# Second block's attention over even and odd tokens, four heads in a row

## The chip, the cores and the metric

One core of one Trainium2 chip runs the program. The metric is the device time of one execution in microseconds; of several executions the median is given. Shorter is better.

## What is computed

The program computes two transformer-like blocks over one sequence of 256 tokens of width 1024. The change touches only the second block's attention: three groups of 8 heads (head size 64), each with its own window and dilation.

```python
DILATED_GROUPS = ((128, 1), (512, 4), (2048, 16))      # (window, dilation)

def dilated_window_attention(q, k, v, window, dilation):
    """query t attends keys t, t-d, ..., t-(window//d)*d"""

def hybrid_mixer(x, w_in, conv_w, conv_b, conv_ln_g, conv_ln_b, w_attn_out, w_conv_out, w_o):
    h = x @ w_in
    ...
    gates = jax.nn.sigmoid(h[..., QKV_COLS + 2 * CONV_CHANNELS:])
    g_attn, g_conv = jnp.split(gates, 2, axis=-1)
    for g, (window, dilation) in enumerate(DILATED_GROUPS):
        q = apply_rotary(qkv[:, :, g, 0], cos, sin)
        k = apply_rotary(qkv[:, :, g, 1], cos, sin)
        o, lse = dilated_window_attention(q, k, qkv[:, :, g, 2], window, dilation)
    ...                                   # the groups are joined by softmax over lse
    y_attn = o.reshape(B, S, ATTN_WIDTH) @ w_attn_out
    u = a * jax.nn.sigmoid(b)             # a, b: the rest of h
    u = conv(u) + conv_b                  # 31 taps, one filter per channel
    u = jax.nn.silu(layer_norm(u, conv_ln_g, conv_ln_b))
    y_conv = u @ w_conv_out
    return (g_attn * y_attn + g_conv * y_conv) @ w_o
```

Joining the groups by their log-denominators equals one softmax over the keys of all three groups together, and this is how the kernel computes it. In the second and third group a query sees only keys at a distance that is a multiple of 4 or 16, so an even token sees even tokens alone there and an odd one odd tokens alone.

## The kernel before

Each engine has a program of its own, written in the order in which it runs; semaphores join them. TensorE (PE) multiplies, ScalarE (ACT) applies functions and copies, VectorE (DVE) does arithmetic, GpSimd (POOL) little, SyncE (SP) issues the weight transfers. All products of activations with weights are done in three passes with operands split into a high and a low half: ACT rounds a weight chunk to its high half (L1053, `highs`), DVE subtracts it from the raw one (L1544, `lows`), PE multiplies high with high, high with low and low with high.

A small class (`Psum`) hands out the eight PSUM banks while the programs are written. `take` gives the bank that was handed out longest ago among those allowed (`low` is the lowest allowed, `at` asks for one bank), and returns what must be waited for: the reading of the result that lay there before. So whoever takes a bank waits for the engine that empties it.

The second block first computes its queries, keys and values with `lin_tm` (L459, matmuls L474 to L476): the stationary operand is a slice of 128 tokens of the activations (`hx`), the moving one 512 columns of weights. `turn` rotates q and k on DVE and POOL, PE transposes them (L880), ACT copies them to `Q2` and `K2`.

Then comes a loop of 20 steps, one for each of the 16 pairs (query tile `qb`, head `h`) in `ITEMS2` and four to drain. The query tile 0 is tokens 0 to 127, tile 1 tokens 128 to 255. In step i:

- PE: `scores2` for the heads i and i+1 if i is even (L906): three groups by two heads, of 128 key columns for tile 0 and 256 for tile 1. `turned2(i-3)` (L916): 3 or 6 transposes of the probabilities. `values2(i-5)` if i is odd (L931): 6 or 12 matmuls for two heads. Then the fill of the step: `FILL` holds 16 gate projections (24 matmuls each, L384 to L389) for steps 0 to 15 and 8 of `conv_out` (12 each) from step 16 on, the last two of them after the loop. In steps 4, 8 and 9 there are small matmuls for the convolution's layer norm (L939, L527, L533).
- ACT: `pt2(i-3)` copies the transposed probabilities out of PSUM (L1420), `exps2(i)` (L1414) applies exp and sums, then `highs` of a later weight chunk (L1053) and the tanh of the gate (L1406), which frees its bank.
- DVE: `maxes2(i)` adds the mask and takes the maximum (L2120), then scales it by -0.125 (L2123); `norm2(i-1)` (L2130, L2132) divides by the sum; in the first steps the rest of the convolution taps (L2077); `lows` of a later chunk (L1544); parts of the layer norm (`rstd` L1585 to L1589 in step 8) and for `conv_out` L2143.

```python
    for i in range(20):
        if i < 16 and i % 2 == 0:
            scores2(i)
        if 0 <= i - 3 < 16:
            turned2(i - 3)
        if i >= 5 and i % 2:
            values2(i - 5)
        ...
        for what, m in fills(i):
            (gate if what == "gate" else conv_out)(m, None if i < 8 or i > 15 else 6 if i < 13 else 7)
```

The output of a query tile gathers in one PSUM bank (`o2`, held from h = 0 to h = 6) and is split by ACT (`out2`, L1425) and DVE (L2137). Behind the loop PE projects it (`ao`, L968 to L970), DVE merges with the gates (L2212, L2215, L2206), ACT rounds (L1477), and PE goes on with `w_o` (L367 to L371).

The first block's attention, in `layer`, has a loop of its own, with scores of four heads in a row in the banks 0 to 3, `turned` (L781) with 4 transposes for each item of its second layer, and `values` (L796) for two heads at a time with 8 matmuls for each pair.

Of the kernel before, what the change touches and what calls it, by code (L numbers as in the profile page):

```python
# [31 lines left out]
def const_layout():  # L32
# [8 lines left out]
        ("mask1", 3 * 256),  # L41
# [163 lines left out]
def geometry(K):  # L205
# [64 lines left out]
    g.P2 = area(4 * 768)  # L270
    g.rot = g.P2
    g.P2T = area(4 * 768)
# [73 lines left out]
def tensor_program(K, e):  # L346
# [112 lines left out]
    def lin_tm(key, wname, l, cols, n, xh, xl, tiles, per, xw, side=None, mid=None, chunk=1):  # L459
# [4 lines left out]
        for g in range(0, KD, per):  # L464
# [418 lines left out]
    for gi in range(3):  # L883
        for w in range(3):
            last = (gi, w) == (2, 2)
            lin_tm(("qkv", gi, w), "w_in_2", 0, (gi * 1536 + w * 512, 512), 512, x2h, x2l, [0, 1], 2, xt, mid=heads2 if last else None, chunk=2)
            if late:
                heads2()
            if w < 2:
                late.append((gi, w))  # L890

    def gate(m, at):
        lin(("gate", m), "w_in_2", 0, (4608 + 1024 + P * m, P), range(KD), x2h, x2l, 256, xt, at)

    def conv_out(m, at=None):
        lin(("cout", m), "w_conv_out_2", 0, (P * m, P), range(4), lambda k: K.ch[:, k, :], lambda k: K.cl[:, k, :], 256, lambda k: V["ch", k], at)

    def scores2(i):

        qb, h = ITEMS2[i]  # L900
        w = (qb + 1) * P
        pe.wait_ge(A["heads2"], *(x for y in range(2) for x in ps.take(("s2", i + y), 1 + qb, at=2 * y if qb else None)))
        for gi in range(3):
            for y in range(2):
                r = slice(64 * y, 64 * y + 64)
                n = e.matmul(ps.ap(("s2", i + y), w, gi * w), g.Q2[r, gi, h // 2, qb * P:(qb + 1) * P], g.K2[r, gi, h // 2, 0:w], start=True, stop=True, skip_group_check=True)  # L906
        n.then_inc(*M.up(("s2", i)))

    def turned2(i):
        qb = ITEMS2[i][0]  # L910
        n = 3 * (qb + 1)
        key = ("p2T", i)
        pe.wait_ge(V["p2", i], *ps.take(key, 1 + qb, at=4 if qb else None))
        for j in range(n):
            o = i % 4 * 768 + j * P
            k = e.transpose(ps.ap(key, P, j * P), g.P2[:, o:o + P], C("ident"))  # L916
        k.then_inc(*M.up(key))

    def values2(i):

        qb, h = ITEMS2[i]
        nb = qb + 1
        key = ("o2", qb)
        if h == 0:
            pe.wait_ge(*ps.take(key, hold=True, at=7 - qb))
        pe.wait_ge(A["p2t", i + 1], A["v2"])
        for j in range(3 * nb):
            for y in range(2):
                o = ps.ap(key, P, (h // 2) * P, slice(64 * y, 64 * y + 64))
                pt = (i + y) % 4 * 768 + j * P  # L930
                n = e.matmul(o, g.V2[:, j % nb, j // nb, (h + y) * 64:(h + y + 1) * 64], g.P2T[:, pt:pt + P], start=j == 0, stop=j == 3 * nb - 1, skip_group_check=True)  # L931
        n.then_inc(*M.up(("pv2", i)))
        if h == 6:
            M.mark(key)
            ps.drop(key)
# [5 lines left out]
    for i in range(20):  # L941
        if i < 16 and i % 2 == 0:
            scores2(i)
        if 0 <= i - 3 < 16:
            turned2(i - 3)
        if i >= 5 and i % 2:
            values2(i - 5)
# [7 lines left out]
        for what, m in fills(i):  # L955
            (gate if what == "gate" else conv_out)(m, None if i < 8 or i > 15 else 6 if i < 13 else 7)
# [84 lines left out]
def scalar_program(K, e):  # L1041
# [367 lines left out]
    def exps2(i):  # L1409
        w = 3 * (ITEMS2[i][0] + 1) * P  # L1410
        z = i % 4
        pb = g.P2[:, z * 768:z * 768 + w]
        ac.wait_ge(V["max2", i])
        e.activation(pb, pb, ACT.Exp, bias=g.st2[:, z:z + 1], scale=0.125, accum_out=g.st2[:, 4 + z:5 + z]).then_inc(*A.up(("exp2", i)))  # L1414

    def pt2(i):
        n = 3 * (ITEMS2[i][0] + 1) * P
        y = i % 4
        ac.wait_ge(M["p2T", i], M["pv2", (i - 4) // 2 * 2] if i >= 4 else None)
        e.activation(g.P2T[:, y * 768:y * 768 + n], ps.ap(("p2T", i), n), ACT.Copy).then_inc(*A.up(("p2t", i)))  # L1420
        ps.give(("p2T", i), A.now())

    def out2(qb):
# [1228 lines left out]
```

## Time and profile before

| | |
|---|---|
| median of 3 runs | 871.27 us (869.71 to 871.9) |
| the profiled execution, its own time | 870.63 us |
| its span, first to last instruction | 868.7 us |
| PE busy | 845.6 us (97%) |
| DVE busy | 624.5 us (72%) |
| ACT busy | 446.9 us (51%) |
| mean granted TensorE clock | 0.996 of full speed |

The span is what the profile explains; 1.9 us of the execution's time lie around it. PE is nearly always busy, so what counts is PE's work in a stage and the places where PE waits. The loop of 20 steps runs from 545.37 us to 633.46 us of the span. Shapes in the rows are partitions x elements; in the profile each matmul of attention in plain fp32 (L906, L931, L796) stands as two records, so 6 matmuls are "x12".

### The profile page before, as it was taken

The numbers are of one execution on the slowest core, as the hardware profiler recorded it, in microseconds if no ns is written. First come the engines' busy times: TensorE is split into PE (matmuls) and PEld (weight loads), VectorE is DVE, ScalarE is ACT, GpSimd is POOL, SyncE is SP. The second block draws the span as 40 slices with busy tenths as digits, with TensorE's granted clock in tenths as the row PEclk, the third lists the DMA queues.
The fourth block names the chain that finished last, engine by engine and source line by source line (L and its number), as shares of the span: only waits on it lengthen the run. The fifth ranks groups of instructions, "written<-read, shape, count | busy, mean of one in ns | idle before, by whom it ended". The sixth has DMA issues, their size and how long they took to land.

```text
span 868.7 us, 13531 instructions
## 1 busy us (share of the span) xinstructions
PE 845.6 (97%) x5432; PEld 701.5 (81%) x5432; DVE 624.5 (72%) x1242; ACT 446.9 (51%) x782; POOL 23.4 (3%) x19
## 2 busy tenths in 40 slices
PE   7999999999999999999999999999999999999996
PEld 4668567776876888769988888998999988888885
DVE  4544867867456779875699999977598766565665
ACT  3352636645433565764444444666653765555552
POOL 0000000000000000000003113000000000000000
PEclk9999999999999999999999999999999999999999
DMA  9785542301173035222655665532456365655541
GB/s 353 311 309 194 218 182 97 110 2 61 62 276 117 24 106 175 74 98 97 215 182 164 197 199 163 167 123 60 127 190 236 105 209 172 213 170 193 195 168 49
DMA packets 40718, 138.27 MB, mean 159 GB/s; under 512 B 4432, under 2 KB 4560, under 8 KB 40400
## 3 DMA queue, kind: packets, MB, share of 16 engines
q1 hardware_dynamic: 40224, 134.41, 45.7%
q10 hardware_dynamic: 432, 3.00, 0.9%
q8 instruction: 43, 0.70, 0.3%
q14 instruction: 19, 0.16, 0.1%
HBM read 136.34 MB, written 1.05 MB: 158 GB/s over the span
## 4 chain that ended last, share of the span: by engine, by line
PE 83%; DVE 8%; DMA 3%; ACT 3%; issue 1%; SPq 1%; POOLq 0%; DVEq 0%; POOL 0%; ACTq 0%
PE ps L429 9%; PE ps L1013 6%; PE ps L384 5%; PE ps L385 5%; PE ps L474 5%; PE ps L476 5%; PE ps L475 5%; PE ps L430 4%; PE ps L389 4%; PE ps L773 2%; PE ps L781 2%; DMA AF<-wmod 2%; PE ps L796 2%; DVE wlo L1544 2%; PE ps L504 2%; PE ps L401 2%
## 5 line engine op out<-in xcount | busy, mean ns | idle before, releaser
L1053 ACT ACTIVATE whi<-raw 128x1024 fp32r<-128x1024 f32 (+3 forms) x213 | 211.6, 1003 | 102.2 <-DMA raw<-wpack 56.4
L1544 DVE TENSOR_TENSOR wlo<-raw,whi 128x1024 fp32r<-128x1024 f32 (+3 forms) x213 | 240.9, 1154 | 27.5 <-ACT whi L1053 27.3
L384 PE MATMUL ps<-hx,whi 128*128 128x256 f32 (+1 forms) x384 | 115.5, 301 | 0.0
L429 PE MATMUL ps<-hx,whi 128*128 128x512 f32 x320 | 113.8, 398 | 0.0
L385 PE MATMUL ps<-hx,whi 128*128 128x256 f32 (+1 forms) x384 | 112.1, 292 | 0.0
L389 PE MATMUL ps<-hx,wlo 128*128 128x256 f32 (+1 forms) x332 | 97.0, 292 | 0.0
L430 PE MATMUL ps<-hx,wlo 128*128 128x256 f32 x320 | 89.8, 281 | 0.0
L384 PEld LDWEIGHTS ps<-hx,whi 128*128 128x128 f32 x384 | 73.4, 191 | 3.4 <-issue 1.9
L385 PEld LDWEIGHTS ps<-hx,whi 128*128 128x128 f32 x384 | 73.5, 191 | 2.0 <-issue 0.7
L474 PE MATMUL ps<-whi,hx 128*128 128x512 f32 (+1 forms) x192 | 71.8, 374 | 0.9 <-DVE lat L1680 0.9
L429 PEld LDWEIGHTS ps<-hx,whi 128*128 128x128 f32 x320 | 60.2, 188 | 14.5
L475 PE MATMUL ps<-wlo,hx 128*128 128x512 f32 (+1 forms) x192 | 71.0, 370 | 0.0
L476 PE MATMUL ps<-whi,hx 128*128 128x512 f32 (+1 forms) x192 | 71.0, 370 | 0.0
L389 PEld LDWEIGHTS ps<-hx,wlo 128*128 128x128 f32 x332 | 63.5, 191 | 1.1
L430 PEld LDWEIGHTS ps<-hx,wlo 128*128 128x128 f32 x320 | 60.5, 189 | 0.7
L2077 DVE SCALAR_TENSOR_TENSOR AF<-AF,cst 128x256 f32<-128x256 f32 x120 | 58.1, 532 | 0.4
L1013 PE MATMUL ps<-whi,hx 128*128 128x512 f32 x176 | 51.2, 392 | 0.0
L1301 ACT ACTIVATE AF<-ps,AF 128x512 f32<-128x512 f32 (+1 forms) x48 | 29.2, 613 | 29.0 <-DVE AF L1956 29.0
L474 PEld LDWEIGHTS ps<-whi,hx 128*128 128x128 f32 x192 | 36.7, 191 | 6.6 <-DVE lat L1680 1.1
L2297 DVE TENSOR_TENSOR AF<-AF,ps 128x256 f32<-128x256 f32 x20 | 8.4, 422 | 45.8 <-ACT AF L1514 45.8
L476 PEld LDWEIGHTS ps<-whi,hx 128*128 128x128 f32 x192 | 36.7, 191 | 5.6
L475 PEld LDWEIGHTS ps<-wlo,hx 128*128 128x128 f32 x192 | 36.8, 192 | 5.4
(326 smaller groups left out, 1649.4 us busy)
## 6 DMA issues: line engine op xcount, KB each, us to landing
raw<-wpack SPq DMA_DIRECT2D x181, 512.0 KB, 4.0
AF<-wmod SPq DMA_DIRECT2D x48, 512.0 KB, 6.4
raw<-wpack SPq DMA_DIRECT2D x24, 256.0 KB, 3.4
raw<-wpack SPq DMA_DIRECT2D x6, 384.0 KB, 3.4
XT<-xin SPq DMA_DIRECT2D x4, 512.0 KB, 6.2
raw<-wpack SPq DMA_DIRECT2D x4, 432.0 KB, 5.0
cst<-cpack ACTq DMA_DIRECT2D x1, 1349.0 KB, 9.0
AF<-l2rows ACTq DMA_DIRECT2D x1, 1024.0 KB, 6.8
```

The lines of the kernel that those rows point to most:

```text
L384: e.matmul(o, wh[:, b], xh(k), start=j == 0, stop=False, skip_group_check=True)
L385: e.matmul(o, wh[:, b], xl(k), start=False, stop=False, skip_group_check=True)
L389: e.matmul(o, wl[:, b], xh(k), start=False, stop=False, skip_group_check=True)
L429: e.matmul(ps.ap(key, 512).rearrange("p (s n) -> p s n", s=2), wh[:, b], K.hx[:, :, k, 0:256], start=k == 0, stop=False, skip_group_check= ...
L430: i = e.matmul(ps.ap(key, 256), wl[:, b], hh[:, k, 0:256], start=False, stop=k == KD - 1, skip_group_check=True)
L474: e.matmul(o, xh(k)[:, ts], wh[:, b], start=k == 0, stop=False, skip_group_check=True)
L475: e.matmul(o, xh(k)[:, ts], wl[:, b], start=False, stop=False, skip_group_check=True)
L476: i = e.matmul(o, xl(k)[:, ts], wh[:, b], start=False, stop=k == KD - 1, skip_group_check=True)
L1013: i = e.matmul(ps.ap(("fd", t), 512, 512 * q), y[:, f % 8, x], w[:, 512 * q:512 * q + 512], start=f == 0 and y is K.fh and w is wh, stop=f ...
L1053: e.activation(W.hi(i), W.raw(i), ACT.Copy).then_inc(*HI.up(j))
L1544: e.tensor_tensor(W.lo(i), W.raw(i), W.hi(i), ALU.subtract).then_inc(*LO.up(j))
L2077: e.scalar_tensor_tensor(out=g.CV[:, m, :], in0=g.U[:, m, j:j + 256], scalar=w, in1=g.CV[:, m, :], op0=ALU.mult, op1=ALU.add).then_inc(*V. ...
```

## The change

Queries are taken as even tokens (tile t = 0) and odd tokens (t = 1), and so are keys: `lin_tm` gets `parity=True` for q, k and v and loads every second column of the activations as its stationary operand. In the second and third group a query needs only the keys of its own parity, in the first group all 256. Every item so has 256 + 128 + 128 = 512 key columns, where it had 384 for the first tile and 768 for the second. The scores of an item fit in one bank.

- `scores2` now does four heads in a row (12 matmuls), in steps 0, 4, 8 and 12, always into the banks 0 to 3. All else takes the banks 4 to 7 (`ps.low = 4`) until step 14.
- `turned2` has 4 transposes and follows one step later (i-4).
- `values2` has 8 matmuls for two heads; two calls stand together in the steps 8, 12, 16 and 19. The output is gathered for four heads in a bank and split four times (`out2(0)` to `out2(3)`), written to every second column of `oh` and `ol`.
- DVE takes four maxima in a row; the scaling by -0.125 goes into the same instruction (scale -0.125 and minimum), so L2123 goes. `norm2(i)` follows in the same step. ACT's exponentials and copies get the order of the first block's loop.
- `P2` has 8 buffers of 512 instead of 4 of 768. The masks take 640 columns in place of 768 in the constants, and the rotary tables are laid out by parity.

```diff
@@ lin_tm
-                    ts = slice(t * P, (t + 1) * P)
+                    ts = slice(t, 2 * P, 2) if parity else slice(t * P, (t + 1) * P)
...
     def scores2(i):
-        qb, h = ITEMS2[i]
-        w = (qb + 1) * P
-        pe.wait_ge(A["heads2"], *(x for y in range(2) for x in ps.take(("s2", i + y), 1 + qb, at=2 * y if qb else None)))
-        for gi in range(3):
-            for y in range(2):
...
+        t, h = ITEMS2[i]
+        pe.wait_ge(A["heads2"], *(x for j in range(4) for x in ps.take(("s2", i + j), at=j)))
+        for gi, at, n, first in ((0, 0, 256, 0), (1, 256, P, t * P), (2, 384, P, t * P)):
+            for j in range(4):
+                r = slice(64 * (j % 2), 64 * (j % 2) + 64)
+                m = e.matmul(ps.ap(("s2", i + j), n, at), g.Q2[r, gi, (h + j) // 2, t * P:(t + 1) * P], g.K2[r, gi, (h + j) // 2, first:first + n], start=True, stop=True, skip_group_check=True)
...
     def turned2(i):
-        pe.wait_ge(V["p2", i], *ps.take(key, 1 + qb, at=4 if qb else None))
-        for j in range(n):
+        pe.wait_ge(V["p2", i], *ps.take(key))
+        for j in range(4):
...
     def values2(i):
+        key = ("o2", i // 4)
+        if h % 4 == 0:
+            pe.wait_ge(*ps.take(key))
         pe.wait_ge(A["p2t", i + 1], A["v2"])
-        for j in range(3 * nb):
+        for j, (u, gi) in enumerate(((0, 0), (1, 0), (t, 1), (t, 2))):
...
     for i in range(20):
-        if i < 16 and i % 2 == 0:
+        ps.low = 4 if i < 15 else 0
+        if i < 16 and i % 4 == 0:
             scores2(i)
-        if 0 <= i - 3 < 16:
-            turned2(i - 3)
-        if i >= 5 and i % 2:
-            values2(i - 5)
+        if i >= 8 and i % 4 == 0:
+            values2(i - 8)
+            values2(i - 6)
+        if 0 <= i - 4 < 16:
+            turned2(i - 4)
+        if i == 19:
+            values2(12)
+            values2(14)
@@ scalar_program
-        if 0 <= i - 3 < 16:
-            pt2(i - 3)
-        if i < 16:
-            exps2(i)
+        for j in ((i, i + 1), (i + 1,), (i + 1,), ())[i % 4] if i < 16 else ():
+            exps2(j)
+        for j in ((), (i - 5,), (i - 5,), (i - 5, i - 4))[i % 4]:
+            if j >= 0:
+                pt2(j)
...
-        if i == 12:
-            out2(0)
+        if i in (8, 12, 16):
+            out2(i // 4 - 2)
@@ vector_program, maxes2
-        e.tensor_tensor_reduce(p3, s3, mk, 1.0, -3.0e38, ALU.add, ALU.max, mx).then_inc(*V.up())
+        e.tensor_tensor_reduce(p2, s2, mk, -0.125, 3.0e38, ALU.add, ALU.min, g.st2[:, z:z + 1]).then_inc(*V.up(("max2", i)))
         ps.give(("s2", i), V.now())
-        dv.wait_ge(V.now())
-        e.tensor_scalar(mx, mx, -0.125, None, ALU.mult, ALU.bypass).then_inc(*V.up(("max2", i)))
@@ vector_program, the loop
+        for j in range(i, i + 4) if i < 16 and i % 4 == 0 else ():
+            maxes2(j)
         if i < 16:
-            maxes2(i)
-        if 0 <= i - 1 < 16:
-            norm2(i - 1)
+            norm2(i)
```

Where the instructions stand. First ACT in the steps 4 and 5, before the change (L1420 is the copy `pt2`, L1414 the exponential, L1429 the mean, L1053 a high half, L1406 the tanh of a gate):

```order
L1420 ACTIVATE AF<-ps 128x384 [waits mm_done]
L1414 ACTIVATE AF<-AF 128x384 [waits dve_done]
L1429 ACTIVATE acc<-ps 128x256 [waits mm_done]
L1053 ACTIVATE whi<-raw 128x1024 [waits raw_in3]
L1406 ACTIVATE AF<-ps 128x256 [waits mm_done]
L1420 ACTIVATE AF<-ps 128x384 [waits mm_done]
L1414 ACTIVATE AF<-AF 128x384 [waits dve_done]
L1053 ACTIVATE whi<-raw 128x1024 [waits raw_in0]
L1406 ACTIVATE AF<-ps 128x256 [waits mm_done]
```

and in the changed kernel (L1413 is the exponential, L1418 the copy `pt2`, L1428 the mean):

```order
L1413 ACTIVATE AF<-AF 128x512 [waits dve_done] x2
L1428 ACTIVATE acc<-ps 128x256 [waits mm_done]
L1053 ACTIVATE whi<-raw 128x1024 [waits raw_in3]
L1406 ACTIVATE AF<-ps 128x256 [waits mm_done]
L1413 ACTIVATE AF<-AF 128x512 [waits dve_done]
L1418 ACTIVATE AF<-ps 128x512
L1053 ACTIVATE whi<-raw 128x1024 [waits raw_in0]
L1406 ACTIVATE AF<-ps 128x256 [waits mm_done]
```

Before, a step's copy came ahead of its exponential, and the copy of one item fell in the same step as its transposes. Now the exponential stands ahead of the copy, and the copy falls in the step after the transposes of its item, behind the tanh of the gate of that earlier step.

Next PE at the start of step 5 of the changed kernel: the last matmuls of the gate of step 4, the transposes, and the first matmuls of the gate:

```order
L385 MATMUL ps<-hx,whi 128x256
L387 MATMUL ps<-hx,wlo 128x256
L913 MATMUL ps<-cst,AF 128x128 [waits act_done]
L913 MATMUL ps<-cst,AF 128x128 x3
L384 MATMUL ps<-hx,whi 128x256 [waits act_done,w_low]
L385 MATMUL ps<-hx,whi 128x256
```

The gate of step 5 waits for ACT here: it takes the bank in which `turned2(0)` of step 4 lay. The gate of step 10 has the same wait, for the bank of `turned2(5)` of step 9. Then step 8 as a whole up to its gate (L905 is `scores2`, L927 `values2`, L913 `turned2`):

```order
L905 MATMUL ps<-AF 128x256 [waits dve_done]
L905 MATMUL ps<-AF 128x256 x3
L905 MATMUL ps<-AF 128x128 x8
L927 MATMUL ps<-AF 64x128 [waits act_done]
L927 MATMUL ps<-AF 64x128 x7
L927 MATMUL ps<-AF 64x128 [waits act_done]
L927 MATMUL ps<-AF 64x128 x7
L913 MATMUL ps<-cst,AF 128x128 [waits dve_done]
L913 MATMUL ps<-cst,AF 128x128 x3
L527 MATMUL ps<-cst,acc 128x1 [waits dve_done]
L527 MATMUL ps<-cst,acc 128x1
L384 MATMUL ps<-hx,whi 128x256 [waits act_done,w_low]
```

and the same step before:

```order
L906 MATMUL ps<-AF 128x256 [waits dve_done,act_done]
L906 MATMUL ps<-AF 128x256 x5
L916 MATMUL ps<-cst,AF 128x128 x3
L527 MATMUL ps<-cst,acc 128x1 [waits dve_done]
L527 MATMUL ps<-cst,acc 128x1
L384 MATMUL ps<-hx,whi 128x256 [waits act_done,w_low]
```

The scores of four heads and the values of four heads now stand in one step; the step after it has the transposes alone, with a wait for DVE (the bank of the output), and the small matmul of the layer norm with a wait for ACT (the bank of `turned2(4)`). Step 9 on PE in the changed kernel, with the end of the gate ahead of it and the start of its own:

```order
L385 MATMUL ps<-hx,whi 128x256
L387 MATMUL ps<-hx,wlo 128x256
L913 MATMUL ps<-cst,AF 128x128 [waits dve_done]
L913 MATMUL ps<-cst,AF 128x128 x3
L533 MATMUL ps<-wk,cst 128x256 [waits act_done]
L384 MATMUL ps<-hx,whi 128x256 [waits w_low]
```

The gate of step 9 has no wait for a bank left; the two waits stand ahead of it.

## Rows read from the trace of the kernel before

**Rows 1.** Busy time of the engines in the loop: us, then each engine's
```profile
545.37:633.46 88.09, 87.90 (x802) 81.97 (x801) 66.95 (x164) 54.68 (x106) 0.00 (x0) 1.00 0.38 120
```

**Rows 2.** The chain that ended last, 540 to 650: start, us, engine and line
```profile
540.00 0.23 PE ps L475
...
545.43 0.87 PE ps L906 x12
...
576.63 1.50 PE ps L906 x12
...
630.78 0.42 DVE AF L2143
631.20 0.60 DVE hx L2137
631.80 1.13 DVE wlo L1544
...
647.64 0.43 ACT hx L1477
```

**Rows 3.** PE in order of time, second gate of the loop: start, us
```profile
549.21 0.28 PE L384 MATMUL ps<-hx,whi 128*128 128x256 f32 x1
...
552.18 0.94 PE L906 MATMUL ps<-AF 64*128 64x128 f32 x12
```

**Rows 4.** PE in order of time, first block's second attention
```profile
363.88 0.60 PE L781 MATMUL ps<-cst,AF 128*128 128x128 f32 x4
364.24 0.36 PE L412 MATMUL ps<-hx,whi 128*128 128x256 f32 x1
364.44 0.28 PE L413 MATMUL ps<-hx,wlo 128*128 128x256 f32 x1
...
372.56 1.97 PE L796 MATMUL ps<-AF 128*64 128x128 f32 x32
374.46 0.66 PE L781 MATMUL ps<-cst,AF 128*128 128x128 f32 x4
374.87 0.36 PE L401 MATMUL ps<-hx,whi 128*128 128x256 f32 x1
```

**Rows 5.** DVE in order of time, in the loop
```profile
547.00 0.56 DVE L2120 CUSTOM_DVE_ANT_1 AF<-ps,cst 128x384 f32<-128x384 f32 x1
547.48 0.08 DVE L2120 DVE_READ_ACCUMULATOR2_ANT AF<- 128x1 f32 x1
547.60 0.15 DVE L2123 TENSOR_SCALAR AF<-AF 128x1 f32<-128x1 f32 x1
547.67 2.46 DVE L2077 SCALAR_TENSOR_TENSOR AF<-AF,cst 128x256 f32<-128x256 f32 x6
550.05 1.22 DVE L1544 TENSOR_TENSOR wlo<-raw,whi 128x1024 fp32r<-128x1024 f32 x1
...
578.17 0.96 DVE L2120 CUSTOM_DVE_ANT_0 AF<-ps,cst 128x768 f32<-128x768 f32 x1 [2.60 <-PE ps L906]
...
579.77 0.15 DVE L1585 TENSOR_SCALAR nrm<-ps 128x2 f32<-128x2 f32 x1
...
581.68 1.22 DVE L1544 TENSOR_TENSOR wlo<-raw,whi 128x1024 fp32r<-128x1024 f32 x1
```

**Rows 6.** ACT in order of time, in the loop
```profile
564.06 0.37 ACT L1406 ACTIVATE AF<-ps 128x256 f32<-128x256 f32 x1
564.37 0.49 ACT L1420 ACTIVATE AF<-ps 128x384 f32<-128x384 f32 x1
564.76 0.61 ACT L1414 ACTIVATE AF<-AF 128x384 f32<-128x384 f32 x1
565.27 0.19 ACT L1414 ACTIVATION_READ_ACCUMULATOR AF<-AF 128x1 f32 x1
565.36 1.05 ACT L1053 ACTIVATE whi<-raw 128x1024 fp32r<-128x1024 f32 x1
```

**Rows 7.** Line 474, its weight loads: ns min/median/max, first and last start
```profile
L474 PEld LDWEIGHTS ps<-whi,hx x192: 186/188/329, 69.6 to 544.4; 128*128 128x128 f32 x192
```

More of the change, by code:

```diff
@@ L919, in values2 @@
     def values2(i):
[L921 to L925, printed above, removed]
+        t, h = ITEMS2[i]
+        key = ("o2", i // 4)
+        if h % 4 == 0:
+            pe.wait_ge(*ps.take(key))
         pe.wait_ge(A["p2t", i + 1], A["v2"])
-        for j in range(3 * nb):
+        for j, (u, gi) in enumerate(((0, 0), (1, 0), (t, 1), (t, 2))):
             for y in range(2):
-                o = ps.ap(key, P, (h // 2) * P, slice(64 * y, 64 * y + 64))
-                pt = (i + y) % 4 * 768 + j * P
-                n = e.matmul(o, g.V2[:, j % nb, j // nb, (h + y) * 64:(h + y + 1) * 64], g.P2T[:, pt:pt + P], start=j == 0, stop=j == 3 * nb - 1, skip_group_check=True)
+                o = ps.ap(key, P, (h // 2) % 2 * P, slice(64 * y, 64 * y + 64))
+                pt = (i + y) % 4 * 512 + j * P
+                n = e.matmul(o, g.V2[:, u, gi, (h + y) * 64:(h + y + 1) * 64], g.P2T[:, pt:pt + P], start=j == 0, stop=j == 3, skip_group_check=True)
         n.then_inc(*M.up(("pv2", i)))
-        if h == 6:
+        if h % 4 == 2:
             M.mark(key)
-            ps.drop(key)
     def conv_sums():
@@ L955, in tensor_program @@
         for what, m in fills(i):
-            (gate if what == "gate" else conv_out)(m, None if i < 8 or i > 15 else 6 if i < 13 else 7)
+            (gate if what == "gate" else conv_out)(m)
     M.mark("attn2")
@@ L1468, in scalar_program @@
                 gate(m)
-    out2(1)
+    out2(3)
     for what, m in FILL[22:]:
@@ L2132, in norm2, with out2 @@
         e.tensor_scalar(pb, pb, sm, None, ALU.mult, ALU.bypass).then_inc(*V.up(("p2", i)))
-    def out2(qb):
-        dv.wait_ge(A["o2", qb])
-        c = slice(qb * P, (qb + 1) * P)
-        e.tensor_tensor(K.ol[:, :, c], ps.ap(("o2", qb)).rearrange("p (k n) -> p k n", k=4), K.oh[:, :, c], ALU.subtract).then_inc(*V.up("o2"))
-        ps.give(("o2", qb), V.now())
+    def out2(q):
+        dv.wait_ge(A["o2", q])
+        k, ts = slice(q % 2 * 2, q % 2 * 2 + 2), slice(q // 2, 2 * P, 2)
+        e.tensor_tensor(K.ol[:, k, ts], ps.ap(("o2", q), 256).rearrange("p (k n) -> p k n", k=2), K.oh[:, k, ts], ALU.subtract).then_inc(*V.up("o2"))
+        ps.give(("o2", q), V.now())
     def conv_out(m):
@@ L2558, in tables, with mask @@
     ang2 = (np.arange(256, dtype=f32)[:, None] * inv2[None]).astype(f32)
-    c["cos2"] = np.cos(ang2).astype(f32).reshape(2, 128, 32).transpose(1, 0, 2)
-    c["sin2"] = np.sin(ang2).astype(f32).reshape(2, 128, 32).transpose(1, 0, 2)
+    c["cos2"] = np.cos(ang2).astype(f32).reshape(128, 2, 32)
+    c["sin2"] = np.sin(ang2).astype(f32).reshape(128, 2, 32)
     c["nsin2"] = -c["sin2"]
-    t, s = np.arange(256)[:, None], np.arange(256)[None, :]
-    m = []
-    for win, dil in ((128, 1), (512, 4), (2048, 16)):
-        ok = (t >= s) & ((t - s) % dil == 0) & ((t - s) <= win)
-        m.append(np.where(ok, 0.0, NEG).astype(f32))
-    c["mask1"] = np.stack([x[128:, :] for x in m], 1)
+    def mask(a, b, win, dil):
+        t, s = 2 * np.arange(128)[:, None] + a, 2 * np.arange(128)[None, :] + b
+        return np.where((t >= s) & ((t - s) % dil == 0) & (t - s <= win), 0.0, NEG).astype(f32)
+    near = (128, 1)
+    c["mask1"] = np.stack([mask(1, 0, *near), mask(0, 0, *near), mask(0, 1, *near), mask(0, 0, 512, 4), mask(0, 0, 2048, 16)], 1)
     e = np.zeros((128, 4), f32)
```

62 lines of the change are left out of this document (27 added, 35 removed).

## Prediction

> **What bounds the kernel now.** I read first the busy times of the loop that the change rewrites: PE is busy 87.90 of its 88.09 us [rows 1], while DVE works 66.95 and ACT 54.68. So a matmul taken out of the loop is worth its full length, as long as nobody makes PE wait in its place. Then the chain that ended last [rows 2]: through the loop it is PE's own work; it leaves PE at 630.78, where DVE takes up the sixth `conv_out`, and stays on DVE up to 647.6 (the split of the output 0.60, low halves of 1.13, the merging), before ACT and PE's `w_o`. DVE's stretch starts from a result of PE, so what the loop gains or loses on PE is passed on whole. Then PE in order of time [rows 3, 4] for lengths of blocks, and DVE and ACT in order of time [rows 5, 6], because they empty the banks that PE takes.
>
> **PE's work after the change.** I build the new loop from blocks, each from the start of a block to the start of the next. Scores: 6 matmuls of 128 columns take 0.87, of 256 columns 1.50 [rows 2], so 0.145 and 0.25 each; a row of four heads is 4 x 0.25 + 8 x 0.145 = 2.16, four rows 8.6. Values: the first block already has exactly the new block (two pairs, 8 matmuls each, x32): 374.46 - 372.56 = 1.90 [rows 4]; four of them 7.6. Transposes: four in a row take 0.36 between projections, 0.41 behind values [rows 4]; 11 and 5 of them make 6.0. Projections: one gate with the switch to scores behind it took 552.18 - 549.21 = 2.97 [rows 3]; 24 matmuls at 0.12 are 2.88 of it and 0.09 is the switch. 16 gates and 8 `conv_out` of half the length are 57.6. The first projection matmul behind another kind takes 0.20 [rows 4] in place of 0.12: 17 such switches are 1.4. Seven switches into scores and values are 0.6. The three small groups of the layer norm stay as they are; what is left of the 88.09 once all old blocks are taken off gives them about 1.1 with their switches (0.33, 0.37 and 0.42, my division). Sum: 8.6 + 7.6 + 6.0 + 57.6 + 1.4 + 0.6 + 1.1 = 82.9. PE's work falls by 88.1 - 82.9 = **5.2 us**.
>
> **What PE then waits for.** Before, PE could take any bank; now steps 0 to 14 have four banks (4 to 7) for a transpose result, a gate, and now and then an output or a statistic. A bank comes back after four takes. In two steps this gives the gate of step i the bank of the transposes of step i-1: step 5 (bank of item 0) and step 10 (bank of item 5). The copy that empties it is on ACT, in step i, behind the tanh of the gate before and an exponential. ACT's prices [rows 6], start to start: tanh 0.27 to 0.31, exponential 0.51 + 0.09 at 384 columns (I take 0.72 at 512), copy 0.39 at 384 (0.50 at 512, both raised with the columns), high half 1.05 long, 0.95 to the next. DVE's [rows 5]: a maximum at 384 columns runs 0.48 and 0.12 more until its result can be used; at 768 its duration is 0.96 in place of 0.56, so at 512 one takes 0.61 + 0.12 = 0.735, four 2.95. The removed L2123 gives 0.07 of start to start.
>
> *Step 10*: the gate of step 9 ends at a time T. ACT sees it at T + 0.2 (a matmul lasts 0.28, and T is 0.12 from the last one's start [rows 3]), then tanh 0.27, exponential 0.72, copy 0.50, and 0.1 to PE: T + 1.8. PE has only four transposes (0.36) to do meanwhile. It waits **1.4**.
>
> *Step 5*: DVE is behind here. Before, it worked the six last taps (2.38) and a low half after one maximum; now it starts at 547.6 (first row of scores done, 545.37 + 2.16 + 0.1), and does 4 maxima 2.95, norm 0.59, taps 2.38, low 1.13, then norm, four taps 1.6, low, then norm, sums 1.6, low, then norm, low: it comes to the maxima of step 4 at 563.1, though PE has had those scores ready since 561.4. ACT: exponentials of items 4 and 5 from 563.9 to 565.3, mean 0.27, high half 0.95, tanh to 566.8, exponential of item 6 to 567.5, copy of item 0 to 568.0, PE at 568.1. PE comes there at 545.37 + 2.16 + 2.97 + 3 x 2.88 + 0.09 + 2.15 + 0.41 + 0.33 + 2.97 + 0.36 = 565.4. It waits **2.7**. Without DVE's delay it would be the 1.4 of step 10; that is the lower bound.
>
> *Step 9*: the transposes want the bank of the first output, which DVE empties only behind four maxima (2.95), norm 0.59 and the `rstd` of 1.91 (581.68 - 579.77 [rows 5]) and 0.36 for the split: 5.9 after the scores are seen. PE has values 1.90, transposes 0.41, the statistic 0.37 and a gate 2.97 = 5.65: it waits **0.4**. Behind it the layer norm's matmul wants the bank of item 4: T + 1.8 again, against 0.4 + 0.36 done: **1.0**. Sum of waits: 2.7 + 0.4 + 1.0 + 1.4 = **5.5 us**. In step 19 item 15's transposes stand next to the values that need them; its copy (0.50 and about 0.3 to see and be seen) is covered by `values2(12)` (0.95). Its bounds are 0 and 0.4; I take 0, as the copy before it is done by then.
>
> **Balance.** PE: -5.2 + 5.5 = +0.3. The DVE stretch behind the loop is shorter by the half of the split, 0.60 [rows 2] to about 0.35, but then meets PE's second `ao` result some 0.2 early: about -0.05 net. DVE's removed work (some 3 us) and ACT's are on no path, as both wait for PE often. The smaller constants transfer is not on the path either. I round to +0.4: 870.63 + 0.4 = 871.0 for the profiled execution; the median of before stands 0.64 above it, so 871.7.
>
> **The strided load.** q, k and v load every second column as stationary operand, 432 times (9 x 8 x 2 x 3). No load of before is strided. The nearest row is the packed load of the same place: 188 ns [rows 7], while a matmul follows another every 0.23 us [rows 2], so a load may grow by 40 ns and cost nothing. Bounds: 0 below (a strided read has no reason to be faster, and it is covered), above a load twice as long, 376 ns, which shows 376 - 230 = 146 ns each time: 63 us. I take 0, as the nearest row has the cover. The Trainium skill, "Advanced Engine Details and Errata", section "Memory Cachelines", says that SBUF is read in lines of 16 bytes, that two accesses to the same line are needed for full speed, and that a new line with every access costs. Every second fp32 value is two accesses a line, so by this rule there is no penalty; with its single-access case it would be my upper end. No run here shows it yet.
>
> **Rivals.**
> (a) *The waits are smaller*: DVE is less behind in step 5, or the copy comes sooner. For it: all of these are short ACT instructions; against: the order on ACT is fixed, 1.4 in step 10 is there whatever DVE does. With 1.4 in step 5 and none on the output's bank: 5.2 - 3.8 = 1.4 won, 869.9.
> (b) *The banks do not bind at all*, because a wait falls on a bank that is free: the whole 5.2 is won, 866.1. Against: the waits for ACT stand in the order of PE's instructions in exactly the steps 5, 9 and 10.
> (c) *The strided load shows*. It decides from 230 ns a load on, and costs 0.43 us for each further nanosecond: 250 ns would give 880, twice the load 935. For: nothing like it in the trace. Against: the cover and the rule.
> (d) *DVE's bundles starve more*: the low half for the fourth gate comes at 554.7 where PE wants it at 556.3, only 1.6 of room; and four maxima in a row put off `rstd` in step 8, whose result PE wants 0.4 after it is there by my sum. If DVE is 1 us later throughout, all waits but that of step 10 grow by it: +2.5 to +3, about 874.5. Slower, but less than (c).
>
> **Chances.** My forecast, 871.7, has 0.66; (a) 0.12; (b) 0.06; (c) 0.06; (d) 0.10. A measurement of this kernel tells about 0.3%, 2.6 us, from no change. Faster by more: (b) and a third of (a): 0.10. Slower by more: (c) and three quarters of (d): 0.13. The same: 0.77. Range: my forecast with (a) and most of (d), and some spread of three-run medians (869.7 to 871.9 before): 869.5 to 874.5; (b) and (c) and a rest of (d) are left out.
>
> **What would show it.** Right: in the loop PE's busy time near 83 in place of 87.9, and idle time on PE of 4 to 6 us before L384 (steps 5 and 10), the transposes and L533 in step 9, released by ACT's copy (L1418) and by DVE. The loop's length 88 to 89. Loads of L474 to L476 below 230 ns and their matmuls still 0.23 apart. DVE idle before the maxima of steps 8 and 12 as before. Wrong: PE idle below 3 us in the loop, (b) or (a); the q, k, v stage longer than before, (c); idle PE before L384 released by DVE's low halves, (d).

## The result and the profile after

The changed kernel takes 875.01 us (median of 11 executions, 872.91 to 878.18); the kernel before 870.88 (median of 11, of which three are those of the forecast). The ratio, from executions side by side, is 1.0055, interval [1.0043, 1.0066]: slower by 4.8 us by this ratio, by 4.1 by the two medians. Forecast were 871.7 and a range of 869.5 to 874.5. The profiled execution has a span of 872.7 against 868.7.

The busy times of the changed kernel in four stretches: the q, k and v products from the first to the last of them, the step from there to the first scores, the loop, the rest. The columns are us, then each engine's busy us (PE, PE's weight loads, DVE, ACT, GpSimd), the granted clock (1.00 is full speed), the busy share of the DMA engines and their GB/s:

```profile
440.50:546.52 106.02, 106.02 (x481) 88.50 (x480) 103.00 (x171) 46.01 (x52) 20.98 (x12) 1.00 0.58 182
546.52:548.09 1.57, 0.40 (x2) 0.00 (x0) 0.90 (x3) 1.08 (x2) 0.00 (x0) 1.00 0.67 198
548.09:637.39 89.30, 84.40 (x776) 81.21 (x777) 63.19 (x146) 51.28 (x106) 0.00 (x0) 0.98 0.36 111
637.39:872.70 235.31, 226.78 (x1336) 199.49 (x1334) 158.17 (x253) 124.85 (x201) 2.24 (x3) 0.99 0.51 172
```

The same four of the kernel before (the third is that of [rows 1]):

```profile
441.89:545.05 103.16, 103.16 (x482) 85.90 (x480) 101.98 (x169) 46.16 (x52) 21.00 (x12) 1.00 0.59 184
545.05:545.37 0.32, 0.32 (x3) 0.01 (x1) 0.32 (x1) 0.00 (x0) 0.00 (x0) 1.00 0.12 51
545.37:633.46 88.09, 87.90 (x802) 81.97 (x801) 66.95 (x164) 54.68 (x106) 0.00 (x0) 1.00 0.38 120
633.46:868.70 235.24, 226.76 (x1336) 199.57 (x1334) 158.54 (x253) 124.94 (x201) 2.24 (x3) 0.99 0.52 173
```

So the time went to three places: +2.86 in the products, where PE is busy all the time in both kernels; +1.25 in the step into the loop; +1.21 in the loop, at a mean granted clock of 0.98 where before had 1.00. The rest behind the loop is 0.07 longer. Ahead of 440 the changed kernel happened to be 1.39 earlier; that part varies from execution to execution (the first of the products stood at 440.5 to 443.7 in the profiles of this study). In this pair a fall of the clock goes a long way to explain it: before's TensorE was at half clock from 83.1 to 86.5, which is 1.7 us of full speed lost, and the changed kernel's was not.

*The products.* The weight loads of line 474 (count, busy us, mean ns), to be held against [rows 7]:

```profile
L474 PEld LDWEIGHTS ps<-whi,hx 128*128 128x128 f32 x144 | 27.9, 194 | 5.4
```

The median was 188 ns there and is 193 here. By my sum a load up to 230 ns costs nothing. Yet 432 matmuls take 2.86 us more, 6.6 ns each.

*The step into the loop.* PE in order of time, then ACT:

```profile
546.52 0.40 PE L476 MATMUL ps<-whi,hx 128*128 128x512 f32 x1
548.09 0.70 PE L905 MATMUL ps<-AF 64*128 64x256 f32 x4 [1.18 <-ACT AF L1400]
```
```profile
546.96 1.08 ACT L1400 ACTIVATE AF<-ps 128x512 f32<-128x512 f32 x2 [1.21 <-PE ps L476]
```

The first row of scores now takes banks 0 to 3 by number. Bank 2 holds half of the last V product, which ACT can copy out (L1400) only after the last matmul. Before, the first scores took other banks, and L906 followed L476 after 0.32.

*The loop.* Who waited for whom between 540 and 640 (us in total, times, longest), the lines on PE, and the longest on its weight loads (PEld):

```profile
PEld ps L384 <- DVE wlo L1544: 4.3, 2, 2.8
PE ps L384 <- ACT AF L1418: 3.9, 2, 2.6
...
PE ps L905 <- ACT AF L1400: 1.2, 1, 1.2
PE ps L533 <- ACT AF L1418: 1.0, 1, 1.0
```

The lines on PE are, but for the 1.2 of the entry (L905), the waits that I had forecast in steps 5 and 10 (L384) and 9 (L533), for the bank that ACT's copy (L1418) empties. The chain that ended last goes through them, where it lay on PE before [rows 2]. From 550.2 to 566.3 it lies on DVE but for 1.0, so step 5 inherits DVE's lateness, as forecast; then it is ACT's:

```profile
566.31 1.55 ACT AF L1413 x4
568.12 0.94 ACT whi L1053
569.34 0.70 ACT AF L1413 x2
570.04 0.49 ACT AF L1418
```

Behind the longest of them comes what I had not forecast. The windows are the transposes and the wait of step 5, the gate's group behind it, and the step after:

```profile
567.50:570.67 3.17, 0.60 (x6) 0.38 (x5) 3.06 (x9) 3.17 (x9) 0.00 (x0) 1.00 0.38 143
571.60:574.80 3.20, 3.20 (x17) 3.20 (x16) 3.17 (x6) 0.00 (x0) 0.00 (x0) 0.50 0.49 170
575.20:578.20 3.00, 3.00 (x28) 3.00 (x27) 1.50 (x5) 2.89 (x9) 0.00 (x0) 1.00 0.82 268
```
```profile
571.46 0.36 PE L384 MATMUL ps<-hx,whi 128*128 128x256 f32 x1
571.62 0.42 PE L385 MATMUL ps<-hx,whi 128*128 128x256 f32 x1
571.83 0.42 PE L389 MATMUL ps<-hx,wlo 128*128 128x256 f32 x1
```

PE had been idle for 2.6 us up to 570.67 (0.6 us of transposes ahead of that) and had worked again for 0.9; then the granted clock is 0.50, that is 1.2 GHz in place of 2.4, from 571.5 to 574.9. The matmuls follow each other after 0.21 in place of 0.12, and the gate takes 4.44 in place of 2.95: +1.5.

### The profile page after: what moved, and what is told of

Read it like the earlier page. It is cut to its first block, busy times and chain, and to the rows that moved or that the text cites. A ratio compares the mean times of both kernels' runs of the same rounds, so it can differ in the third digit from the quotient of the medians.

```text
span 872.7 us, 13452 instructions
## 1 busy us (share of the span) xinstructions
PE 843.8 (97%) x5408; PEld 701.8 (80%) x5408; DVE 621.8 (71%) x1228; ACT 444.4 (51%) x784; POOL 23.4 (3%) x19
## 4 chain that ended last, share of the span: by engine, by line
PE 81%; DVE 9%; DMA 4%; ACT 4%; issue 1%; SPq 1%; POOLq 0%; DVEq 0%; POOL 0%; ACTq 0%
PE ps L429 9%; PE ps L1013 6%; PE ps L384 5%; PE ps L474 5%; PE ps L385 5%; PE ps L476 5%; PE ps L475 5%; PE ps L430 4%; PE ps L389 4%; DMA AF<-wmod 3%; PE ps L773 2%; PE ps L781 2%; PE ps L796 2%; DVE wlo L1544 2%; PE ps L401 2%; PE ps L412 2%
## 5 line engine op out<-in xcount | busy, mean ns | idle before, releaser
L1053 ACT ACTIVATE whi<-raw 128x1024 fp32r<-128x1024 f32 (+3 forms) x213 | 211.7, 1004 | 103.2 <-DMA raw<-wpack 39.3
L384 PE MATMUL ps<-hx,whi 128*128 128x256 f32 (+1 forms) x384 | 115.7, 301 | 3.9 <-ACT AF L1418 3.9
L384 PEld LDWEIGHTS ps<-hx,whi 128*128 128x128 f32 x384 | 74.1, 193 | 6.6 <-DVE wlo L1544 4.3
L476 PE MATMUL ps<-whi,hx 128*128 128x512 f32 (+1 forms) x192 | 71.0, 370 | 0.0
L476 PEld LDWEIGHTS ps<-whi,hx 128*128 128x128 f32 x192 | 36.9, 192 | 5.8
```

What stands on the lines that cost most here:

```text
L384: e.matmul(o, wh[:, b], xh(k), start=j == 0, stop=False, skip_group_check=True)
L476: i = e.matmul(o, xl(k)[:, ts], wh[:, b], start=False, stop=k == KD - 1, skip_group_check=True)
L1053: e.activation(W.hi(i), W.raw(i), ACT.Copy).then_inc(*HI.up(j))
```

## The experiments

Each ratio is to the kernel before on the same chip, whose median was 870.33 beside contiguous loads, strided loads alone, scores' banks and early copy (the first chip), 870.70 beside gathered, banks and copy, 18 zeros and all three (the second), 870.16 beside the rest (the third). So medians of different rows can come from different chips. Edits that add lines move the line numbers behind them by a few (L2133 for L2132, for instance). Measured in the profiles, stretch by stretch: the products from the first to the last, the step to the first scores, the loop up to the first `ao` product.

| run | median us | ratio to before | products | step | loop |
|---|---|---|---|---|---|
| before | 870.88 | 1 | 103.16 | 0.32 | 88.09 |
| changed | 875.01 | 1.0055 [1.0043, 1.0066] | 106.02 | 1.57 | 89.30 |
| changed again | 876.12 | 1.0072 [1.0052, 1.0091] | 106.02 | 1.57 | 87.80 |
| contiguous loads | 872.57 | 1.0026 [1.0011, 1.0041] | 103.17 | 1.56 | 87.80 |
| strided loads alone | 873.21 | 1.0036 [1.0022, 1.005] | 106.02 | 0.33 | 88.08 |
| every fourth column | 876.94 (one) | | 107.40 | 1.57 | 89.32 |
| gathered by GpSimd | 872.52 | 1.0022 [1.0008, 1.0036] | 103.16 | 1.57 | 89.30 |
| scores' banks | 874.69 | 1.0047 [1.0029, 1.0065] | 106.02 | 0.32 | 87.80 |
| early copy | 869.67 | 0.9996 [0.9983, 1.0009] | 106.02 | 1.57 | 83.71 |
| banks and copy | 869.63 | 0.999 [0.997, 1.001] | 106.02 | 0.32 | 83.71 |
| 18 zeros in the wait | 878.97 | 1.0097 [1.0074, 1.012] | 106.02 | 1.57 | 92.79 |
| 6 zeros | 875.47 | 1.0057 [1.0043, 1.007] | 106.02 | 1.57 | 87.81 |
| all three | 866.33 | 0.9951 [0.9935, 0.9967] | 103.16 | 0.32 | 83.72 |
| and output early | 865.29 | 0.9954 [0.9942, 0.9967] | 103.16 | 0.31 | 83.71 |

The stretches repeat to 0.02 us, while medians scatter by about 1. What is below that is read from the stretches, one profiled execution each.

### The strided load

Changed kernel, stride taken back; and before, stride alone added:

```diff
-... mid=heads2 if last else None, chunk=2, parity=True)
+... mid=heads2 if last else None, chunk=2)
```


> The changed kernel with one edit taken back: the q, k and v projections load two contiguous halves of the columns again (tokens 0-127, 128-255) instead of every second column. The kernel therefore attends between the wrong tokens; the number and the sizes of all instructions stay. Theory 1 (the load with a stride of two columns costs about 6.7 ns each over 432 loads): 2.9 us faster than the changed kernel, about 872.1 or a ratio to before of 1.002; the stretch of the q, k and v products 103.4 us instead of 106.0, a matmul every 0.227 us instead of 0.2335. Rival (the loads are hidden, the stretch was longer by chance): no change, 875.0, the stretch still at 106.

```diff
-                    ts = slice(t * P, (t + 1) * P)
+                    ts = slice(t, 2 * P, 2) if parity else slice(t * P, (t + 1) * P)
```


> The kernel before with only the strided load of the q, k and v projections added (every second column as stationary operand); all else is before's, so that its masks no longer fit its tokens. Theory 1 (the stride costs 6.7 ns a load): 2.9 us slower than before, ratio 1.0033, loads 193 ns at the median instead of 188. Rival (no cost of the stride): 1.000.

Both came out as theory 1. The products in the first and in the second:

```profile
441.65:544.82 103.17, 103.17 (x482) 85.87 (x480) 101.99 (x169) 46.07 (x52) 21.01 (x12) 1.00 0.56 184
443.26:549.28 106.02, 106.02 (x481) 88.50 (x480) 103.02 (x171) 46.03 (x52) 21.00 (x12) 1.00 0.58 181
```

Step and loop did not move, and the stride alone gives a ratio of 1.0036, an interval clear of 1. The stride costs 2.86 us.

Is it the load that has grown?

```diff
-                    ts = slice(t, 2 * P, 2) if parity else ...
+                    ts = slice(t, t + 4 * P - 3, 4) if parity else ...
...
-... 512, x2h, x2l, [0, 1], 2, xt, ... parity=True)
+... 512, lambda k: hh[:, k, :], lambda k: hl[:, k, :], [0, 1], 2, xt, ... parity=True)
```


> The changed kernel with every fourth column instead of every second as stationary operand of the q, k and v projections (columns 0, 4, ... 508 and 1, 5, ... 509 of the buffer's 512, so half of them are not the block's input): one element in 16 bytes instead of two. Theory A (a load pays for each 16 bytes that it touches, beyond what a contiguous one touches): the stretch of the products grows again, from 106.0 us to 109 or more, loads 206 ns and more. Theory B (any stride costs the same 6 ns, whatever its width): 106.0 us and 194 ns again. Theory C (by the nearest rule of the Trainium skill, Advanced Engine Details and Errata, Memory Cachelines, one hit on a line of 16 bytes is where a penalty begins): a far larger step, a load of 300 ns or more and a stretch of 130 us.

The weight loads of this run over the same stage:

```profile
L474 PEld LDWEIGHTS ps<-whi,hx 128*128 128x128 f32 x144 | 44.6, 310 | 0.0
```
```profile
480.12 0.31 PEld L474 LDWEIGHTS ps<-whi,hx 128*128 128x128 f32 x1
480.36 0.31 PEld L475 LDWEIGHTS ps<-wlo,hx 128*128 128x128 f32 x1
```

None of the three theories holds whole. The load grows from 194 to 310 ns, a step as C said it; A's "206 ns and more" does not exclude it, B does. But the products take 107.40, only 1.38 more than with stride two, where A said 109 or more and C 130: the loads are 310 ns long and begin 0.24 us apart, so they lie over each other. My threshold of 230 ns does not hold, in either direction: 6 ns more a load cost 6.6 ns a matmul, the next 116 ns cost 3.2. The record's length of a load is not what sets the distance of the matmuls. What does was not found.

The stride can be kept out of the loads, with the right tokens:

```diff
+    for k in range(KD):
+        x = K.hx[:, :, k, :]
+        gp.wait_ge(K.mm["go", 2], V["x2", k])
+        e.tensor_copy(x[:, :, 256:512].rearrange("p c (t n) -> p c t n", t=2), x[:, :, 0:256].rearrange("p c (n t) -> p c t n", t=2)).then_inc(*K.pool.up(("x2p", k)))
...
-... 512, x2h, x2l, [0, 1], 2, xt, ... parity=True)
+... 512, lambda k: hh[:, k, 256:512], lambda k: hl[:, k, 256:512], [0, 1], 2, lambda k: K.pool["x2p", k], ...)
```


> The changed kernel, and GpSimd copies the 256 columns of the block's input once, high and low part, into the free half of the same buffer with the even tokens ahead of the odd (8 copies of 128 x 1024 elements, beside the convolution's projections of 23 us), so that the projections load contiguous columns of the right tokens. Theory 1 (the stride costs 2.9 us, wherever the columns come from): 2.9 us faster than the changed kernel, 872.1, loads 188 ns. Rival (GpSimd is late: 12 of its adds of 128 x 512 took 1.75 us each, so eight copies could take 8 x 3.5 = 28 us and more, and the first projection waits; or its accesses slow VectorE): 875 or more, with a wait of PE on GpSimd at 441 to 446.

GpSimd in order of time in this run:

```profile
420.81 5.20 POOL L2350 CAST hx<-hx 128x512 fp32r<-128x512 f32 x8 [420.37 <-PE ps L387]
```

Eight copies take 5.20 us, done long before the first of the products (443.6), and these take 103.16. A copy is 512 elements a partition and not 1024, as I had written, and it is cheaper than the add that the rival was priced from. 872.52 measured, 872.1 expected.

### The banks at the entry

```diff
+self.only = None
-free = [i for i in (range(self.low, 9 - n) if at is None else (at,)) ...
+free = [i for i in (self.only or range(self.low, 9 - n) if at is None else (at,)) ...
-... ps.take(("s2", i + j), at=j)))
+... ps.take(("s2", i + j), at=(0, 1, 3, 6)[j])))
-        ps.low = 4 if i < 15 else 0
+        ps.low, ps.only = 0, (2, 4, 5, 7) if i < 15 else None
```


> The changed kernel with the scores of a row of four heads in banks 0, 1, 3 and 6 instead of 0 to 3, and all else in banks 2, 4, 5 and 7 up to step 14, so that the first row of scores takes no bank in which V still waits for ScalarE's copy. Theory 2 (the entry waits for V's bank): the wait of 1.2 us before the first scores goes, 1.3 us faster than the changed kernel, 873.7, ratio 1.004. Rival (the entry is set by the copies of K and Q or by the maxima behind it): nothing, 875.0, with the same gap before the scores or a later one of the same size at the first transposes.

The step is 0.32 again, the loop behind it unchanged at 87.80: the 1.25 us are won and not given back. The median is 874.69 where 873.7 was expected and the rival said 875.0; on seven executions it cannot tell them apart, so the gain is shown by the stretches alone.

### The late copy

```diff
     for i in range(20):
+        if i >= 4 and i % 4 == 0:
+            pt2(i - 4)
         for j in ((i, i + 1), (i + 1,), (i + 1,), ())[i % 4] if i < 16 else ():
             exps2(j)
-        for j in ((), (i - 5,), (i - 5,), (i - 5, i - 4))[i % 4]:
-            if j >= 0:
-                pt2(j)
+        if i >= 4 and i % 4:
+            pt2(i - 4)
```


> The changed kernel with ScalarE's copy of an item's transposed probabilities in the step of its transposes (ahead of the exponentials in steps 4, 8, 12, behind them in the others) instead of one step later. Theory 3 (the copies come late and hold the bank of a gate's group in steps 5, 9 and 10; behind the wait in step 5 the granted clock falls): the waits of 2.8, 1.2 and 1.5 us shrink to under 1 us together, and with the first of them the stretch at half clock goes: 4.5 to 6.5 us faster than the changed kernel, 868.5 to 870.5, ratio 0.998 to 1.000. Rival A (the copy is late because its transposes are late, and those wait for the maxima and the exponentials): the waits stay, moved to the transposes at most; under 1.5 us faster. Rival B (the clock falls whatever the wait): 3.5 to 5 us faster, and a stretch of 3 us at half clock is still in the loop.

The loop falls from 89.30 in the changed kernel's profile, or 87.80 at full clock, to 83.71, and the time by 5.3 us, as theory 3 had it (4.5 to 6.5). Rival A (under 1.5 us) is out. Rival B, a fall of the clock whatever the wait, is not settled by one profile without the fall. Nor is DVE's low half, named by rival (d) of the prediction, what held PE up, though the profile puts 4.3 us of the weight loads' idle time down to it: DVE's order is untouched here, and the waits are gone. ACT in order of time shows how it goes; the copy of item 0 lies in what had been ACT's wait for DVE's maxima:

```profile
566.75 0.60 ACT L1418 ACTIVATE AF<-ps 128x512 f32<-128x512 f32 x1 [2.16 <-PE ps L913]
568.65 0.72 ACT L1413 ACTIVATE AF<-AF 128x512 f32<-128x512 f32 x1 [1.30 <-DVE AF L2118]
```

PE's busy share of the loop and its one wait of over 0.3:

```profile
550.45:634.16 83.71, 82.43 (x776) 79.69 (x777) 62.96 (x146) 51.30 (x106) 0.00 (x0) 1.00 0.38 118
```
```profile
588.71 0.66 PE L913 MATMUL ps<-cst,AF 128*128 128x128 f32 x4 [1.03 <-DVE hx L2133]
```

Waits of 5.6 us went, and one of 1.03 and one of 0.24 (at the gate of step 13) came. The longer: the transposes of step 9 want the bank of the first output, which DVE empties behind its row of maxima and `rstd`. It is the wait that I had put at 0.4 in the changed kernel; there it did not show, as PE came to it later.

> The changed kernel with both edits, the scores' banks 0, 1, 3, 6 and ScalarE's copy in the step of the transposes. Theory: the two add up: 1.2 us of entry wait and the 5 us of the late copies go, and the granted clock in the loop stays up; about 868.5, ratio 0.998 to before. Rival (with the first wait gone VectorE's bundle of eight maxima is late by as much, so that the transposes of steps 4, 8 and 12 wait longer): about 869.7, as with the early copy alone, with 2 us and more of waits at the transposes.

The loop stays at 83.71 with the entry at 0.32, so the rival falls: what is won at the entry is not given back to the maxima. But the median is 869.63 where 868.5 was expected, equal to that of the early copy alone (869.67, on another chip; this one's interval is the wider), so 1.25 us are shown in the profile and not in the time.

### The clock behind the wait

Zeros multiplied in the wait of step 5, in a bank whose scores DVE had read:

```diff
+        if i == 5:
+            pe.wait_ge(*ps.take(("keep2",), at=0))
+            for _ in range(18):
+                e.matmul(ps.ap(("keep2",), 256), K.zero[:, 0:P], K.zero[:, :], start=True, stop=True, skip_group_check=True)
```


> The changed kernel with 18 matmuls of zeros (256 columns, 0.12 us each, 2.2 us in all) between the transposes and the gate's group of step 5, in the bank of item 4's scores; the late copy and its wait stay, so PE works through most of it. Theory 4 (the wait of 2.8 us in step 5 makes a stretch at half clock more frequent, which is why the mean granted clock of the changed kernel is 0.995 where that of before is 0.996): mean clock back at 0.996 over the runs, 1 us faster than the changed kernel, about 874. Rival (the lower mean clock is chance or has another cause): no change, 875.0, mean clock 0.995.

My price was wrong, and with it the time, 878.97 for the expected 874. The mean granted clock was 0.9970 over 6 executions, as theory 4 had it or above, against 0.9951 over the 11 of the changed kernel on another chip. In this run's order of time the zeros begin at 569.10 and the gate at 576.68:

```profile
569.10 1.46 PE L953 MATMUL ps<-modrow 128*128 128x256 f32 x6
```

18 matmuls took 7.58 us, 0.42 each, so the loop grew by 5.0. Then with `range(6)`, and the changed kernel itself beside it:

> As the filled wait before, but with 6 matmuls of zeros instead of 18: the zeros ran at 0.40 us each, 7.3 us in all, and not at 0.12 as I had taken, so 6 fill 2.4 us of the 2.6. Theory 4 (the wait of step 5 is what lets the clock fall): mean granted clock 0.997, as in the run with 18, against 0.995 of the changed kernel, and about 1 us faster than it. Rival (the clock falls by itself as often): the time and the mean clock of the changed kernel run beside it, within 0.5 us and 0.0005.

> The changed kernel once more, as it is, beside the three others of this call on one chip. Expected by every theory: 875.0, ratio 1.005, the waits at the entry (1.2 us), in step 5 (2.6), step 9 (1.0) and step 10 (1.3) again. Open is the granted clock: if the half-clock stretch behind the wait of step 5 belongs to the kernel, it is there again at about 571 of the span; if it comes and goes, as its absence in two other kernels with the same wait suggests, the profile may lack it and the mean clock of the runs varies between 0.992 and 0.998.

The changed kernel run again waits 2.56 in step 5, and its clock stays at 1.00 in the whole loop, which takes 87.80:

```profile
551.31:639.11 87.80, 82.92 (x777) 79.75 (x777) 63.13 (x146) 51.27 (x106) 0.00 (x0) 1.00 0.35 114
```

The fall in the loop thus comes in some executions only: in three of the six profiles that have the wait (changed, every fourth, gathered), and in none of the eight that have not. But a fall of the same 3.4 us is not peculiar to this wait. The profile of before has one, and so have seven others at about 82 to 87:

```profile
83.10:86.50 3.40, 3.40 (x16) 3.40 (x15) 1.63 (x4) 0.00 (x0) 0.00 (x0) 0.50 0.04 16
```
```profile
79.28 1.84 PE L625 MATMUL ps<-cst,wk 128*128 128x1 f32 x16
80.98 1.03 PE L629 MATMUL ps<-cst,acc 128*128 128x1 f32 x8
```

There PE had no wait; it had worked off 24 records of matmuls with one column, up to 81.87, and 1.2 us of the projections behind them. Two more falls each stand between 12 and 23 in the profiles of "changed again" and "all three". Counted over the whole span up to the last matmul, the six profiles with the wait have seven times 3.4 us at half clock and the eight without it nine times, so by the profiles the wait adds falls in the loop but not in the sum.

The mean granted clock of all executions, says a little more. It counts every fall, and also the end of the span, where half clock costs no matmul anything (in the changed kernel's profile from 868.5 to 872.7). Five runs with the wait (the changed kernel twice) have 0.9948 over 48 executions; seven without it, or with it filled, 0.9963 over 70; before, 0.9961 over 75 (standard errors 0.0002 to 0.0003). A mean lower by 0.0013 is 0.0026 of 870 us at half the clock, in which half the work is done: an estimate of 1.1 us lost on average. It does not stand on every chip: with and without the wait the means are 0.9945 and 0.9962 on the first, 0.9957 and 0.9959 on the second, 0.9937 and 0.9966 on the third. The six zeros gave 875.47 and 0.9962 against 876.12 and 0.9937 of the changed kernel beside them, in the direction of theory 4; but these are 5 and 6 executions, the expected gain was about 1 us, and the profiles of both have no fall in the loop (87.81 and 87.80). So a lower mean clock with the wait is likely, and that the wait makes the fall in the loop is likely too, on three falls; neither is shown.

### What beats both

> The three edits together: the scores' banks, the early copy, and the columns gathered by GpSimd. Theory: 1.2 + 5.2 + 2.9 us off the changed kernel's 875.0, 865.7, ratio to before 0.995. Rival (VectorE's maxima set the loop once the waits are gone, or GpSimd is late): 868 to 870, ratio 0.998 to 1.000.

866.33, ratio 0.9951 [0.9935, 0.9967], where 865.7 was expected. The three terms are in its stretches:

```profile
442.97:546.13 103.16, 103.16 (x481) 85.90 (x480) 101.98 (x169) 46.02 (x52) 21.02 (x12) 1.00 0.56 184
546.13:546.45 0.32, 0.32 (x2) 0.00 (x0) 0.32 (x1) 0.00 (x0) 0.00 (x0) 1.00 0.67 256
546.45:630.17 83.72, 82.44 (x778) 79.70 (x777) 64.35 (x150) 52.45 (x108) 0.00 (x0) 1.00 0.39 125
```

The regrouped attention is worth 4.4 us of loop (88.09 to 83.72) once nobody waits for a late copy. Then the last wait, by moving DVE's `out2` directly behind `norm2(i)`, ahead of `rstd`:

```diff
             norm2(i)
+        if i in (8, 12, 16):
+            out2(i // 4 - 2)
...
-        if i in (8, 12, 16):
-            out2(i // 4 - 2)
```


> All three edits, and on VectorE the subtraction that frees the output's bank moved ahead of the layer-norm's row work in steps 8, 12 and 16. Theory (item 5's transposes in step 9 wait 1.03 us for that bank alone): the wait goes, 1.0 us faster than the three edits, 865.3, ratio 0.994. Rival (the transposes then wait for item 5's normalised probabilities, which are late behind the same work): no change, 866.3, and a wait of the same size on the probabilities.

The theory fell. PE in order of time, step 9:

```profile
585.18 0.70 PE L533 MATMUL ps<-wk,cst 128*128 128x256 f32 x2 [0.99 <-DVE wk L1590]
```

The wait for the bank is gone, and one of 0.99 for the result of `rstd` stands behind it: DVE does the same work before both. The rival had the size right and named another instruction. The loop is 83.71 as without the edit; the median is lower by 1.04 on another chip, and the ratio is the same (0.9954 and 0.9951).

## Why the prediction was wrong

**PE's work after the change**: right, 0.7 too high. The loop at full clock takes 87.80, and less the waits (below) 82.2, against 82.9 in my sum. Rows of scores took 1.96, not 2.16: I had divided the old blocks' 0.87 and 1.50 by six, and so took the switch to and from them along twice. Read as 0.105 for every 128 columns and 0.24 once a block, the same two rows give 0.87, 1.50 and 1.92 for the new one. That is 0.8 of the loop. Values were 1.90 as taken from the first block.

**What PE then waits for**: right. By the lengths of the blocks less the 0.35 of four transposes, 2.82 in step 5, 1.26 in step 9 and 1.56 in step 10, 5.6 in all; forecast were 2.7, 1.4 and 1.4, 5.5 in all. Inside step 9 the parts were other ones: nothing on the output's bank, all of it at L533. My 0.4 there was too much by my own figures (5.9 less 5.65 is 0.25), and the sum did not hang on it, as the wait at L533 takes what the first leaves. "Before, PE could take any bank" was not so either: before's `fills` puts the gates of steps 8 to 15 into the banks 6 and 7; no wait followed from it there. Rival (b) was excluded by this, and (a) as well; the early copy shows that 4.1 us of it are avoidable by the order on ACT alone.

**Balance**: +0.3 forecast for the loop, -0.3 measured at full clock; the rest behind it 235.31 against 235.24. This part alone would have been too small to measure in the time.

**The strided load**: this step failed, and it is the largest part of the miss. I took 0, because a load of 188 ns below a matmul every 230 ns seemed to leave 40 ns of cover; it costs 2.86 us at 6 ns more a load. Rival (c) was right that the load shows; its threshold and its price per nanosecond were not. The rule of the Trainium skill, "Advanced Engine Details and Errata", section "Memory Cachelines", by which two accesses a line suffice, comes near: stride two costs 3 in 100 of the load, and the step to 310 ns comes, as the section lets one expect, with one access a line. Full speed at two it is not. That lines are the cause was not tried apart from the stride.

**A wait that I left out**: this step failed too, the step into the loop, put at nothing and 1.25 us long. I had followed the banks from the second take on, and put the start of the first scores at before's 545.37 without asking who held banks 0 to 3. The row for ACT's copies of V stood in the trace, and the change pins these banks by number.

**The granted clock**: left out as well, 1.5 us in the executions that have the fall in the loop; 1.1 on average is the estimate above, which is not shown. My sum priced a wait at its length.

**Rival (d)** named 874.5, close to what came, and not for its reason: DVE came to the maxima of step 4 at 565.58, that is 17.5 behind the first scores, where my sum had 17.7.

Together: 2.86 + 1.25 - 0.29 = 3.8 us from the stretches, and 4.9 with the estimate for the clock, against 4.8 by the ratio and 4.1 by the medians.

## What to carry to other kernels

When a tile gets a fixed bank, look up who holds that bank at its *first* use, not only in the steady state. Price a changed access pattern by one run of it alone: "covered by the matmul" was no argument here, though the load's record was shorter than the distance of the matmuls. And where each instruction of one engine stands a step late, that costs nothing until the buffers between two engines get fewer; then moving it one step forward can be worth more than the change itself (4.1 us of the loop here, by an edit of a few lines).

## What the hardware showed that I had not expected

- A weight load with every second fp32 column takes 194 ns in place of 188 and moves the matmuls 6.6 ns apart; with every fourth, 310 ns, and 3.2 ns more. Loads of 310 ns followed each other after 0.24 us.
- A wait of 2.6 us on PE was followed by 3.4 us at half the clock in some executions, not in others of the same kernel. The same length at half the clock stood behind 2.6 us of one-column matmuls without any wait, in eight of fourteen profiles, that of before among them.
- A matmul of 256 columns took 0.42 us from the buffer of zeros, declared fp32, and takes 0.12 in the projections, whose operands are fp32r. In the profile each of the former stands as two records, the latter as one. Whether the type is the cause was not tried.
- A GpSimd copy of 128 x 512 took 0.65 us, its adds of the same size 1.29 to 2.2, 1.75 on average.
